# A TensorE wait for its own finished matmuls, before the fourth slot of the last up projection

## The reference, cut to what matters

```
z = modulate(rmsnorm(h, ffn2_norm_g[l]), m[6], m[7])
gate, up = split(z @ ffn2_w_in[l], 2)          # 1024 -> 2 x 2816
h = h + 0.5 * m[8] * ((silu(gate) * up) @ ffn2_w_out[l])
return rmsnorm(h, final_norm_g)
```

## Time and profile before

| | |
|---|---|
| median of three runs | 1560.94 us (1560.77 to 1561.71) |
| the profiled execution | 1560.44 us, of which the span of the profile is 1558.7 us |
| matmul side of TensorE | busy 1538.1 us (99%), 8844 matmuls |
| VectorE, ScalarE, GpSimd | busy 67%, 44%, 10% |
| from slot 3 of the last up projection to the last matmul of the down projection | 171.47 us, 1512 matmuls |

### The profile page before, as it was taken

The page is one execution under the profiler, slowest core; times in us unless marked ns, Lnnn a source line. Parts: engine busy times, 40 slices in busy tenths (PEclk is TensorE's granted clock), DMA queues, the critical chain, the costliest instruction groups (busy, mean ns, idle before and its releaser), DMA issues.

```text
span 1558.7 us, 22174 instructions
## 1 busy us (share of the span) xinstructions
PE 1538.1 (99%) x8844; PEld 1319.3 (85%) x8844; DVE 1048.0 (67%) x1297; ACT 678.2 (44%) x1104; POOL 159.2 (10%) x189
## 2 busy tenths in 40 slices
PE   8999999999999999999999999999999999999997
PEld 6888888889878988888888898888888896999997
DVE  6777874794868577874378477875358669975553
ACT  4434433333684343433233352433333359664552
POOL 0011110022000201101002200011002211000011
PEclk9999999999999999999999999999999999999999
DMA  9577664674422257663367437674357525456562
GB/s 369 203 210 206 206 182 134 211 209 129 136 82 70 93 176 204 206 184 105 115 202 218 123 124 215 203 213 117 96 189 232 160 90 156 151 190 195 189 208 89
DMA packets 77228, 264.64 MB, mean 170 GB/s; under 512 B 9424, under 2 KB 9680, under 8 KB 76112
## 3 DMA queue, kind: packets, MB, share of 16 engines
q1 hardware_dynamic: 69456, 250.80, 49.9%
q0 software_dynamic: 7680, 12.59, 5.0%
HBM read 247.62 MB, written 1.05 MB: 160 GB/s over the span
## 4 chain that ended last, share of the span: by engine, by line
PE 94%; DVE 2%; ACT 1%; DMA 1%; issue 0%; SPq 0%; POOL 0%; POOLq 0%; DVEq 0%; ACTq 0%
PE bank L454 85%; PE bank L576 2%; PE bank L582 2%; PE bank L578 2%; DMA ada_head<-head_w 1%; PE bank L717 1%; PE bank L742 1%; PE bank L719 1%; PE bank L718 1%; PE bank L531 0%; DVE w_lo L1161 0%; PE bank L470 0%; PE bank L462 0%; DVE l_q L1423 0%; DVE l_bx L1430 0%
## 5 line engine op out<-in xcount | busy, mean ns | idle before, releaser
L871 ACT ACTIVATE w_hi<-raw 128x1024 fp32r<-128x1024 f32 x317 | 336.0, 1060 | 717.2 <-PE bank L454 699.7
L1161 DVE TENSOR_TENSOR w_lo<-raw,w_hi 128x1024 fp32r<-128x1024 f32 x317 | 389.6, 1230 | 312.6 <-ACT w_hi L871 312.0
L454 PE MATMUL bank<-z_hi,w_hi 128*128 128x512 f32 (+1 forms) x1480 | 534.7, 361 | 1.7 <-DVE w_lo L1161 1.3
L454 PE MATMUL bank<-z_lo,w_hi 128*128 128x512 f32 (+1 forms) x1480 | 532.3, 360 | 0.0
L454 PE MATMUL bank<-z_hi,w_lo 128*128 128x512 f32 (+1 forms) x1480 | 532.1, 360 | 0.0
L454 PEld LDWEIGHTS bank<-z_hi,w_hi 128*128 128x128 f32 x1480 | 278.2, 188 | 51.3 <-issue 5.9
L454 PEld LDWEIGHTS bank<-z_hi,w_lo 128*128 128x128 f32 x1480 | 278.1, 188 | 42.5
L454 PEld LDWEIGHTS bank<-z_lo,w_hi 128*128 128x128 f32 x1480 | 278.2, 188 | 42.0
L454 PE MATMUL bank<-h_hi,w_hi 128*128 128x512 f32 (+1 forms) x770 | 266.1, 346 | 0.0
L454 PE MATMUL bank<-h_hi,w_lo 128*128 128x512 f32 (+1 forms) x770 | 265.6, 345 | 0.0
L454 PE MATMUL bank<-h_lo,w_hi 128*128 128x512 f32 (+1 forms) x770 | 265.6, 345 | 0.0
(11 more groups left out here) (177 smaller groups left out, 1383.8 us busy)
## 6 DMA issues: line engine op xcount, KB each, us to landing
raw<-weights SPq DMA_DIRECT2D x320, 512.0 KB, 3.9
ada_raw<-ada_w SPq DMA_DIRECT2D x128, 512.0 KB, 4.3
ada_head<-head_w SPq DMA_DIRECT2D x8, 1024.0 KB, 18.2
up_acc<-up_acc POOLq DMA_DIRECT2D x20, 256.0 KB, 6.7
down_acc<-down_acc POOLq DMA_DIRECT2D x12, 256.0 KB, 6.1
up_acc<-up_acc POOLq DMA_DIRECT2D x40, 64.0 KB, 5.6
res<-x_t SPq DMA_DIRECT2D x4, 512.0 KB, 5.0
xc_swapped<-xc SPq DMA_DIRECT2D x16, 128.0 KB, 2.4
```

What stands on the lines that cost most here:

```text
L454: m = pe.matmul(bank[:, to], w, x[:, k, at], start=start and i == 0, stop=stop and i == 2, skip_group_check=True)
L871: act.activation(w_hi[:, r, :], raw[:, r, :], ACT.Copy).then_inc(hi_ready, 1)
L1161: dve.tensor_tensor(w_lo[:, r, :], raw[:, r, :], w_hi[:, r, :].bitcast(F32), ALU.subtract).then_inc(lo_ready, 1)
```

## The change

Before slot 3, and only where one stream is left (which is the last up projection alone), TensorE waits until the count of finished slots holds the first three. The program is the same otherwise.

```diff
                 first_slots(n, at["slot"], pa[0:SIDE])
+                if streams(dft(n)) == 1:
+                    pe.wait_ge(slot_done, at["slot"] + SIDE)
                 for p in range(SIDE, 4):
                     slot(0, p)
```

## The result

Over 20 runs of each kernel on one chip the median went from 1561.08 us (1560.53 to 1567.28) to 1565.41 us (1560.78 to 1569.28): a ratio of 1.0021, with a 95% interval from 1.0012 to 1.0030. (The ratios in this document are not quotients of the two medians, which would be 1.0028 here; they lie near the quotient of the means, 1.0020.) The predicted 1567.8 us is 2.4 us above the measured median, which lies inside the predicted range. But of the predicted rise of 0.44% the ratio shows less than half.

The account below looks back on a forecast made before the run. TensorE was taken to bound the kernel. The profiled 1560.44 us + 0.30 (wait) + 6.5 (slow pace) gave 1567.2 us; with 0.5 us from profiled run to median, the forecast was 1567.8 us, range 1560.9 to 1568.4.

Parts of the forecast that it names:

- What bounds the kernel: Whole kernel: TensorE's matmul side is busy 99% of the span, so what TensorE loses comes out at the end.
- The wait itself: Stop before slot 3: its second matmul starts 0.30 us later, bounds 0.2 and 0.5 us.
- What waits behind it: Behind slot 3: only TensorE's later work is held; the supply of `w_lo` has room for the 0.3 us.
- The size of the slow pace: Slot 3 through the down projection: 1512 matmuls at 117.7 instead of 113.4 ns, 6.5 us, bounds 0 and 6.6.
- Rival 2: Slow pace falls back to fast after the up projection (1565.5 us) or at its loop's entry (1561.3 us); chance 0.10.
- That a full stop ends slow: At slot 3: the stop leaves TensorE empty, so the matmuls behind run slow, as after two earlier such stops; 6.5 us.
- the first rival: Only the drain: the stop before slot 3 is short and TensorE stays fast; 1561.2 us, chance 0.29.
- the sign of it: Prediction wrong if other runs of the same kernel differ by some 6 us, the pace then being settled by chance.

Follow-up runs that it names:

- TensorE alone: Separate kernel computing nothing of the model: groups of 24 matmuls behind various starts; of 40 full stops at column 112, 26 ended fast (113.4 ns), 14 slow (117.8 ns).
- the 41 stops: Kernel with TensorE waiting for its own count ahead of each of slots 3 to 43, not slot 3 alone: 1584.69 us, ratio 1.0140 against the kernel before.
- F S S F S S F S: Paces (F 113.4 ns, S 117.8 ns) of eight first groups behind full stops, TensorE alone; same row where 128 or 16 activation-type columns preceded the second groups.
- the satisfied wait: The change's wait at the same place, but for the first two slots alone, whose increments are long given: 1567.45 us, ratio 1.0025 against the kernel before.
- the fourth group: Small matmul within the first three slots: 128 columns with the change 1.0000, 16 columns with it 0.9974, 128 without it 1.0007; the change again, profiled, 1567.88 us.

## Why the prediction was right, and where it was wrong

**What bounds the kernel.** Right: what TensorE lost from slot 3 on came out at the end.

**The wait itself.** Right in kind and nearly in size: 0.25 us for a predicted 0.30, inside its bounds of 0.2 and 0.5. The first load came 0.25 us later relative to the end of line 598, the low edge of what was named; the first matmul stood 0.06 us behind that end, not 0.13, and the second 0.29 us, not 0.33. The restart from another engine's result was a fair stand-in for the restart from TensorE's own.

**What waits behind it.** Right: no idle time of PE behind the stop is put down to `w_lo` or `z_hi`.

**The size of the slow pace.** Right: 6.69 us measured for the predicted 6.5, a little over its upper bound of 6.6, over the whole of the 1512 matmuls. Rival 2 (slow, but not to the end) had no case here; without a new stop the pace passed from slot to slot and on into the down projection in every profile of the change.

**That a full stop ends slow.** This step failed. The prediction put it so: two stops had TensorE stand with nothing in it, both went on slow, and "by the only two rows of that kind the 1512 matmuls would run slow". The runs showed that a full stop ends in either pace: 26 fast and 14 slow with TensorE alone, 17 long and 18 not over the 35 runs of the change (10 of 20, one of one, none of one, one of one, 5 of 12 long). So the forecast of 1567.8 us is right for about half of the runs, the first rival's 1561.2 us for about the other half, and the median fell into the gap. That it came out only 2.4 us from the forecast is luck: with one long run fewer of the 20 it would have been near 1562.5 us. The prediction had named the sign of it, runs of one kernel that differ by some 6 us, but gave it no chance of its own. Read in the rows of before, the five short stops had ended both ways; that was the hint, and two agreeing rows of another kind were too few to set it aside.

With 256 columns at the full clock the runs here show mean distances of 113.4, 117.8, 118.3, 118.5, 118.8 and 120.0 ns, by the place of the activations and, at one place, by what ran before. The Trainium skill ("TensorE: Matmul & The Clock Gate", section "Back-to-back issue gap") gives 262 cycles as the gap of an isolated matmul of 256 columns, by the columns alone (109 ns at the full clock, an estimate worked out from that page of the Trainium skill). The same section of the Trainium skill says that in a stream of weight loads and matmuls, which is what runs here, both set the spacing; it names neither the place of the activations nor two paces, and no run here has the isolated case.

**What the change did to the share of long runs.** On the chip of the result it was 1 of 20 before and 10 of 20 with it. Elsewhere it was 5 of 12 beside 6 of 28, which doesn't tell. Over all chips it is 17 of 35 against 34 of 134 of the kernel before. The share of the kernel before itself differed from group to group, from 1 of 20 to 15 of 29. So that the change makes long runs more frequent is shown for one chip, and how much it does so on another is open.

**What is shown of the cause, and what isn't.** Shown: the long runs of the change are slow by the pace behind the stop (four profiles of the change have the piece of 1512 at 178.35 us, one at 171.65 us); the pace belongs to the place of the activations (column 128: no spread); it comes up without other engines (TensorE alone); its price goes with the matmuls behind it (stop ahead of the down projection); and with one small matmul ahead of slot 4 there are no long runs (0 of 35 in two kernels, one of them run on two chips, where the kernel before on the same chips had 14 of 66).

Not shown: what decides a given stop. A chance drawn at each stop doesn't fit the strict alternation of the 41 stops or the repeated F S S F S S F S. That an empty array is what does it doesn't fit the satisfied wait (10 of 12 long). That the pace is handed on doesn't fit the fourth group. What would fit them all is an outcome that depends on what ran ahead of the stop and on a moment of the restart finer than the trace shows: two profiles of the change with the same pace ahead and starts within 2 ns ended differently. This is an argument; no run here moved the restart finely enough to test it.

**A better version.** The kernel before with one extra matmul ahead of slot 4 has nearly the same fast time and had no long run in 24: in the mean 1561.29 us against 1562.74 (12 and 17 runs), and 1561.12 against 1562.27 (12 and 28 runs). Both intervals of the ratio include 1, and it wasn't run beside the kernel before on the chip where half of that one's runs were slow; there the gain should be larger, which is an argument and not a measurement.

## What to carry to other kernels

Where TensorE bounds a kernel, compare the distance between the starts of equal matmuls along the whole trace: a difference of 4% at the same shape and clock and with no idle time is easy to overlook, and over 1512 matmuls it was some 27 times the cost of the stop that brought it about. A wait on TensorE that looks free, even one that is already satisfied, can change the pace of all that follows it. Look at the single runs before the median, and take two rows that agree for what they are: with outcomes that come half and half, they agree every second time.

## What the runs showed of the hardware that wasn't expected

- Matmuls of 256 columns with new weights each, at the full clock, start 113.3 to 120.0 ns apart by the column at which the activations begin: 112 gives 113.4 or 117.8 ns, 16 and 80 give 117.8, 120 gives 118.3, 96 gives 118.5, 32 gives 118.8, 64 and 128 give 120.0. Only 112 showed two paces, and only there was the fast one seen (the others in six groups each, behind full stops, in one trace); its slow pace is that of 16 and 80, and the other places are slower still.
- A short matmul in the stream can set the pace at column 112 without a stop: 16 or 128 columns of the activations' type gave the slow one (16 of 16, six of them behind a fast group), and 64 columns left it as it was (8 of 8, one of them slow). Behind 128 columns in f32 all 18 groups with TensorE alone were fast, but only one of them stood behind a slow group; that it turns slow into fast is seen there once, and from slot 3 to slot 4 in three profiles of the kernel.
- An additional satisfied wait moved the next load from 0.094 to 0.154 us behind the start of the last matmul, and in the loop, where the trace has one or two register instructions behind the stop, a wait for TensorE's own count added 0.40 to 0.50 us to the stream.
- One program's time on one core can be of two kinds by itself: the share of the slower kind for the same kernel went from 1 of 20 to 15 of 29 from one group of runs to another.
